# Trunk kernel in split float32: split weights of the later blocks loaded by units of 1 MB into three places

## The reference

```python
# even layer
xa, bg, cg, gate_a, u, gate_b = split_cols(rmsnorm(x, g) @ w_in, sizes)   # 1024 -> 6 x 512
ya = short_conv_mixer(xa, bg, cg, conv_w) * silu(gate_a)
yb = pool_mixer(u, pool_w, pool_scale) * silu(gate_b)
x = x + concatenate([ya, yb]) @ w_out
# odd layer
cq, ck, cv, gate_c, dq, dk, dv, di, df, do, gate_d = split_cols(rmsnorm(x, g) @ w_in, sizes)
yc = sliding_window_attention(cq, ck, cv, sinks) * silu(gate_c)     # window 128, 8 heads
yd = mlstm(dq, dk, dv, di + i_bias, df + f_bias) * sigmoid(do) * silu(gate_d)
x = x + concatenate([yc, yd]) @ w_out
return rmsnorm(x, final_norm)
```

## Time and profile before

| | |
|---|---|
| median of 3 runs | 1713.72 us (1711.06 to 1715.32) |
| profiled execution, its own time | 1715.27 us |
| its span, first to last instruction | 1713.5 us |
| TensorE busy | 1673.1 us, 98% |
| weight loads of TensorE (beside its matmuls) | 1390.5 us, 81% |
| VectorE, ScalarE, GpSimd busy | 764.6, 483.2, 332.7 us |
| moved by DMA | 342.69 MB, mean 200 GB/s |
| mean granted clock of TensorE | 0.994 of full speed |

### The profile page before, as it was taken

How to read it: one execution, slowest core, us unless ns; L and a number is a source line. 1 busy time by engine, 2 the same in 40 slices (tenths; PEclk the granted TensorE clock), 3 DMA queues, 4 the chain that set the end, 5 groups by cost and what they waited for, 6 DMA issues and landing times.

```text
span 1713.5 us, 21904 instructions
## 1 busy us (share of the span) xinstructions
PE 1673.1 (98%) x8048; PEld 1390.5 (81%) x8048; DVE 764.6 (45%) x1328; ACT 483.2 (28%) x1153; POOL 332.7 (19%) x463
## 2 busy tenths in 40 slices
PE   6999899999999999999999999999999999999998
PEld 5887787878788888888888878888888888888886
DVE  4645244685423423466442333257543233245752
ACT  2000123462300013356310002336531001243731
POOL 7777664446500000000010000000001000000000
PEclk9999999999999999999999999999999999999999
DMA  8887777657775555544675554644467655554444
GB/s 246 308 293 261 237 249 226 207 166 264 259 263 191 181 167 193 181 132 134 228 247 195 196 174 159 221 148 136 136 233 259 195 188 181 187 177 141 136 159 148
DMA packets 162323, 342.69 MB, mean 200 GB/s; under 512 B 32128, under 2 KB 83840, under 8 KB 162208
## 3 DMA queue, kind: packets, MB, share of 16 engines
q1 hardware_dynamic: 139520, 313.57, 55.1%
q10 hardware_dynamic: 22688, 27.64, 5.1%
HBM read 263.50 MB, written 77.66 MB: 199 GB/s over the span
## 4 chain that ended last, share of the span: by engine, by line
PE 90%; DVE 4%; issue 2%; ACT 2%; DMA 1%; POOL 1%; ACTq 0%; SPq 0%; POOLq 0%; DVEq 0%
PE bank L474 13%; PE bank L476 13%; PE bank L475 13%; PE pair_a L474 5%; PE pair_a L475 5%; PE pair_a L476 5%; PE pair_b L474 4%; PE pair_c L474 4%; PE pair_c L476 4%; PE pair_b L476 4%; PE pair_b L475 4%; PE pair_c L475 4%; PE pair_a L770 2%; PE pair_c L753 1%; PE pair_b L667 1%
## 5 line engine op out<-in xcount | busy, mean ns | idle before, releaser
L474 PE MATMUL bank<-h_hi,slot 128*128 128x512 f32 (+1 forms) x976 | 381.8, 391 | 1.5 <-issue 0.9
L476 PE MATMUL bank<-h_hi,slot 128*128 128x512 f32 (+1 forms) x976 | 377.9, 387 | 0.0
L475 PE MATMUL bank<-h_lo,slot 128*128 128x512 f32 (+1 forms) x976 | 377.6, 387 | 0.0
L474 PEld LDWEIGHTS bank<-h_hi,slot 128*128 128x128 f32 x976 | 184.4, 189 | 39.4 <-issue 2.2
L402 POOL TENSOR_TENSOR rs<-sums,eps 128x1 f32<-128x1 f32 x48 | 9.1, 190 | 1060.3 <-ACT junk L850 1060.3
L476 PEld LDWEIGHTS bank<-h_hi,slot 128*128 128x128 f32 x976 | 184.1, 189 | 37.8
L475 PEld LDWEIGHTS bank<-h_lo,slot 128*128 128x128 f32 x976 | 184.3, 189 | 37.3 <-issue 1.0
L427 POOL TENSOR_TENSOR slot<-stages,slot 128x512 fp32r<-128x512 f32 x132 | 180.5, 1367 | 11.0
L425 POOL TENSOR_SCALAR slot<-stages 128x512 fp32r<-128x512 f32 x132 | 89.5, 678 | 141.8 <-issue 117.8
L474 PE MATMUL pair_a<-h_hi,slot 128*128 128x512 f32 x256 | 101.3, 396 | 0.0
L850 ACT ACTIVATE junk<-res 128x512 f32<-128x512 f32 x64 | 40.5, 632 | 212.8 <-DVE res L1214 165.3
(11 more groups left out here) (285 smaller groups left out, 3172.0 us busy)
## 6 DMA issues: line engine op xcount, KB each, us to landing
slot<-split_weights SPq DMA_DIRECT2D x396, 512.0 KB, 3.3
split_weights<-slot SPq DMA_DIRECT2D x132, 512.0 KB, 4.1
stages<-in_even_w_in SPq DMA_DIRECT2D x48, 256.0 KB, 3.6
stages<-in_odd_w_in SPq DMA_DIRECT2D x36, 256.0 KB, 3.2
result<-res ACTq DMA_DIRECT2D x16, 512.0 KB, 5.8
xin<-in_x ACTq DMA_DIRECT2D x12, 512.0 KB, 7.7
stages<-in_even_w_out SPq DMA_DIRECT2D x16, 256.0 KB, 3.1
stages<-in_odd_w_in SPq DMA_DIRECT2D x32, 128.0 KB, 2.7
```

Of the source, the lines that this page charges most:

```text
L474: t.matmul(dst, l_hi, r_hi, start=start, stop=False)
L475: t.matmul(dst, l_hi, r_lo, start=False, stop=False)
L476: return t.matmul(dst, l_lo, r_hi, start=False, stop=stop)
```

## The change

Two neighbouring slots become one place of 1 MB (`pair`), and a slot is a view of half a place. `load_unit(u)` loads both halves of unit u with one DMA into place u % 3, as soon as both halves of unit u - 3 have been used. TensorE waits for the unit ahead of its first half, and not ahead of the second. The first block, with its four slots filled by GpSimd, stays as it is. There are three semaphores for loads in place of six.

```diff
--- before.py
+++ after.py
@@ -102,7 +102,7 @@
     units += [head_pair_rows(owo, 2 * kp, 512 * n) if kp < 2 else row_unit(owo, 256 * kp, 512 * n)
               for n in range(2) for kp in OOUT_ORDER]
     halves = [half for unit in units for half in unit]
-    assert len(halves) == HALVES and HALVES % SLOTS0 == 0 and HALVES % SLOTS == 0
+    assert len(halves) == HALVES and HALVES % SLOTS0 == 0 and UNITS % 3 == 0
     staged_upto = [16 * sum(len(halves[j]) for j in range(i % STAGES, i + 1, STAGES)) for i in range(HALVES)]
 
     ctx = ExitStack()
@@ -114,7 +114,8 @@
             return ctx.enter_context(nc.semaphore(name))
 
 
-        slots = [sb(f"slot{i}", [P, 2 * HALF], F32R) for i in range(SLOTS)]
+        pair = [sb(f"unit{i}", [P, 2, 2 * HALF], F32R) for i in range(SLOTS // 2)]
+        slots = [pair[i // 2][:, i % 2, :] for i in range(SLOTS)]
         stages = sb("stages", [P, STAGES, HALF])
         stage = [stages[:, i, :] for i in range(STAGES)]
         w_hi = [t[:, 0:HALF] for t in slots]
@@ -220,7 +221,7 @@
         s_split = sem("split")
         s_half = sem("half_unit_done")
         s_saved = [sem(f"split_saved{i}") for i in range(SLOTS0)]
-        s_slot = [sem(f"slot_loaded{i}") for i in range(SLOTS)]
+        s_unit = [sem(f"unit_loaded{i}") for i in range(SLOTS // 2)]
         s_x = [sem(f"x_in{i}") for i in range(TT)]
         s_const = sem("consts")
         s_gain = sem("gain_in")
@@ -328,8 +329,9 @@
                         dst = dst.rearrange("p (k c) -> p k c", k=4)[:, :, c:c + width]
                     sp.dma_start(dst, src).then_inc(s_staged[i % STAGES], 16)
 
-            def load_half(i):
-                sp.dma_start(slots[i % SLOTS][:, :].bitcast(F32), split_dram[i]).then_inc(s_slot[i % SLOTS], 16)
+            def load_unit(u):
+                sp.dma_start(pair[u % 3][:, :, :].bitcast(F32),
+                             split_dram[2 * u:2 * u + 2].rearrange("h p c -> p h c")).then_inc(s_unit[u % 3], 16)
 
             x_rows = x[0]
             for tt in range(TT):
@@ -344,17 +346,17 @@
 
             for i in range(SLOTS0):
                 sp.wait_ge(s_saved[i], 16 * (HALVES // SLOTS0))
-            for i in range(SLOTS):
-                if i < SLOTS0:
-                    sp.wait_ge(s_half, HALVES - SLOTS0 + i + 1)
-                load_half(i)
+            for u in range(3):
+                if u < SLOTS0 // 2:
+                    sp.wait_ge(s_half, HALVES - SLOTS0 + 2 * u + 2)
+                load_unit(u)
             with sp.Fori(1, NB - 1) as b:
-                for i in range(HALVES):
-                    sp.wait_ge(s_half, b * HALVES + i + 1)
-                    load_half((i + SLOTS) % HALVES)
-            for i in range(HALVES - SLOTS):
-                sp.wait_ge(s_half, (NB - 1) * HALVES + i + 1)
-                load_half(i + SLOTS)
+                for u in range(UNITS):
+                    wait_unit(sp, b, u)
+                    load_unit((u + 3) % UNITS)
+            for u in range(UNITS - 3):
+                wait_unit(sp, NB - 1, u)
+                load_unit(u + 3)
 
 
         @block.gpsimd
@@ -499,8 +501,8 @@
 
                     if opening:
                         pe.wait_ge(s_split, i + 1)
-                    else:
-                        pe.wait_ge(s_slot[i % SLOTS], (b - 1) * (16 * (HALVES // SLOTS)) + 16 * (i // SLOTS + 1))
+                    elif i % 2 == 0:
+                        pe.wait_ge(s_unit[i // 2 % 3], (b - 1) * (16 * (UNITS // 3)) + 16 * (i // 6 + 1))
 
                 def chan_half(u, h, dst, part):
```

## The result

The changed kernel takes 1716.8 us (median of 20 runs, 1713.35 to 1719.24), the kernel before 1714.49 us in the same series (20 runs, 1710.48 to 1716.84). The ratio of the two is 1.0017 with a 95% interval of 1.0011 to 1.0024: slower by 2.9 us, between 1.9 and 4.1 (the two medians lie 2.3 us apart). The forecast was 1715.1 us in a range of 1711 to 1719, with 0.88 on a change within 0.3%.

The account below looks back on a forecast made before the run. The prediction took TensorE, busy 1673.1 of 1713.5 us, as the bound. Waits of 1.0 us for unit 0 and 0.4 us for unit 1 added 1.4 us to the median 1713.72, giving 1715.1 us, range 1711 to 1719.

Parts of the forecast that it names:

- the calm: Stretches away from block starts: a unit is loaded 10.9 us ahead of use, so its landing is hidden.
- The price of 1 MB: Landing time of a unit's load after its issue: 3.2 + 1.6 = 4.8 us.
- The lower bound of 3.2: Landing of a 1 MB load if its second half is free: 3.2 us.
- the upper of 6.4: Landing of a 1 MB load if each half pays in full: 6.4 us.
- The few-engines rival: All unit loads: spread over two DMA engines, 26 us per 1 MB, about 5600 us in all; chance 0.01.
- Unit 0: Start of the second block: issued at 456.3, shares engines with the gain load, lands at 463.4; TensorE waits 1.0 us.
- Unit 1 and those behind it: Second block's start: unit 1 lands at 469.3, 0.4 us more wait; units 2 and 4 cause no wait.
- What was said to show the prediction wrong: Calm landings over 6 us, a wait at the third or fourth block's start, or matmul pace other than 0.23 us.
- the signs of being right: A wait of about 1 us near 462 us, calm landings of 4.5 to 5 us, 2.72 us per half unchanged.
- Each half pays in full: Rival at block starts: units land in 6.4 us, adding 12.3 us of waits, 1726 us; chance 0.08 including late broadcast.
- remark on the clock: A TensorE wait of some microseconds could drop its clock, partly to 1.2 GHz; no forecast wait was that long.
- The gate rows: Second block: their broadcasts share the DMA engines, with 2.1 us of room; 0 booked, at most 1 us.

Follow-up runs that it names:

- before_early: The kernel before, with halves 4 and 5 loaded in the middle of the first block's store loop, at half 100; ratio to before 0.9999.
- best_half: The kernel before, with halves 4 and 5 loaded early and TensorE's loop written out as two bodies; 1712.12 us, ratio to before 0.9986.
- after_again: The changed kernel once more, unaltered, for a second trace; ratio to before 1.0019.
- the gain cut: The changed kernel, with the final gain's load at the end of the first three blocks cut to one column; ratio to before 1.0005.
- gain_cut_before: The kernel before, with the final gain's load at the end of the first three blocks cut to one column; ratio to before 0.9994.
- halves_freed: The changed kernel, but each 512 KB half is loaded as soon as it is free, TensorE still waiting for whole units; ratio to before 1.0003.
- waits_back: The changed kernel, with TensorE's wait ahead of every half again; ratio to before 1.0015.
- best_unit: The changed kernel, with unit 2 loaded early and TensorE's loop written out as two bodies; ratio to before 0.9999.
- two_dmas: The changed kernel, but each unit is loaded by two 512 KB DMAs issued together once the whole unit is free; ratio to before 1.0027.

## Why the prediction was right, and where it was not

**The frame held.** TensorE has no wait that a load could take away, the calm hides the larger loads, and the change stays under 0.3%. The forecast 1.4 us against 2.9 measured (1.9 to 4.1) lies within its range, on its side, but too small. That it came so near is in part luck: 1.0 of the 1.4 us was booked for unit 0, where nothing was lost, and 1.2 us was lost at the restart, where nothing was booked.

**The price of 1 MB** was 4.8 us from four loads issued together; measured 4.7 to 5.0. The lower bound of 3.2 and the upper of 6.4 are both out in the calm. The Trainium skill's page "DMA: Bandwidth & Descriptors", section "Bandwidth", has 6.15 us for 1 MB issued from GpSimd; the loads from the SP queue measured here took 4.7 to 5.0 us. The few-engines rival, at 26 us, fell with the landings. The Trainium skill's same page, section "Why a DMA increments its semaphore by 16 and not by 1", gives all sixteen engines for 128 rows outermost; the trace agrees, with a mean of 91% of the sixteen in use while a unit and the gain load were under way.

**Unit 0**: forecast 1.0 us of wait, measured none. It landed at 455.1 + 4.9 = 460.0, 1.2 us ahead of its use. The step that failed is "it shares the engines with the gain load": by the earlier trace rows half 1 had taken 6.2 us, and I put that down to the gain load. But the whole unit, issued 0.9 us ahead of the gain as half 1 was, took hardly more than in the calm. The 6.2 us was no fixed price either: half 1 took 4.3 us in before_early and 5.7 in best_half, each time with the gain load 0.95 us behind it. Why is not shown.

**Unit 1 and those behind it**: forecast 0.4 us for unit 1 and none for 2 and 3; measured 0.84 us over units 1 to 3 in one trace, 1.37 and 1.48 in two more with the same loads, 0.31 with the gain cut. The mechanism is the one named, issue after half 131 into a busy queue. Unit 1 was priced too high: it landed 5.4 us after its issue (6.1 in after_again), against 6.7 in the forecast. Unit 2 was priced right: it landed 11.2 us after the block's first matmul, forecast 473.7 - 462.45 = 11.25. The error was to hide it behind waits of 1.4 us that did not come, so that it landed just at its use. Unit 3 was left out of the list: its second half had landed at 477.3 for a use at 478.8, a room of 1.5 us, and it came 2.2 us later after the block's start than that half had, and not 1.6.

**The term that was missing** is the restart of TensorE's loop, 1.2 us, more than half of the 2.0 us that the trace lost. The earlier trace rows had it in plain sight as 0.9 us "issue", and I took it for no wait on a transfer. It was one: gain_cut_before makes it vanish. **What was said to show the prediction wrong**, a wait at the start of the third block, came true in this form, though no weight load was late there. Of the signs of being right, the calm landings and the 2.72 us per half came as said; the wait of about 1 us near 462 us did not.

**Each half pays in full** (chance 0.08, up to 1726 us) is refuted by the landings in the calm. Its remark on the clock came true sooner than I thought: in two of the traces a step of 2.4 us without a new matmul was followed by the low clock.

**The gate rows**: no wait appeared there; the second block from the 121st matmul on was 387.71 us, against 387.76 before.

## What to carry to other kernels

Where the compute engine never waits for a ring of buffers, larger transfers have nothing to win; they give up the early release of the first half, and that shows first where several transfers meet, at the seams between blocks, and all the more when the ring is short (53 against 15 us of waits with 2 MB of places). Look at such seams one use at a time: time of issue, landing, first use. And read a wait on "issue" at a loop's head as a possible wait for program fetch behind data: writing the loop out, or keeping big transfers away from the jump, is worth a try.

## What the hardware showed that I had not expected

The step at a jump back on TensorE took from 0.23 us, as long as any other step, to 3.34 us. With the full gain load it was 1.05 to 1.39 us where TensorE waited for each half of 512 KB, 2.06 in halves_freed, and 2.40 to 2.44 with loads of 1 MB. Two DMAs of 512 KB issued together on late release did worse than one of 1 MB in the same series (median 1718.73 against 1716.09 us in waits_back), with 30.41 us at the entry of its slowest execution, though one of 1 MB can do as badly (31.15 in best_unit). In two_dmas the second load of unit 1 was issued at 464.1 and landed at 471.5, 7.4 us later, with the stores of the result beside it. And a wait of TensorE of 2.1 us was followed in one execution by 1.2 GHz over several microseconds, while steps of 2.4 us in four others, and of 2.78 and 3.34 us in two_dmas, were not.
